# The second MLP product of a decoder layer as seven block products instead of eight

## What is computed

```
x = _layer_norm(ALPHA * x + mixed, ln1_g, ln1_b)
h = jnp.square(jax.nn.relu(jnp.einsum('bsd,df->bsf', x, w_up)))          # 512 x 4096
x = _layer_norm(ALPHA * x + jnp.einsum('bsf,fd->bsd', h, w_down), ln2_g, ln2_b)
```

## Time and profile before

| | |
|---|---|
| median of 3 runs | 865.61 us (865.6 to 865.99) |
| span of the profiled execution | 865.2 us |
| TensorE busy | 850.2 us (98%), 4185 matmuls |
| VectorE busy | 412.9 us (48%) |
| ScalarE busy | 295.9 us (34%) |
| GpSimd busy | 20.5 us (2%) |
| DMA | 87.42 MB, mean 101 GB/s |
| mean granted TensorE clock | 0.989 of full speed |

### The profile page before, as it was taken

How to read it: one execution, slowest core, us unless ns; L and a number is a source line. 1 busy time by engine, 2 the same in 40 slices (tenths; PEclk the granted TensorE clock), 3 DMA queues, 4 the chain that set the end, 5 groups by cost and what they waited for, 6 DMA issues and landing times.

```text
span 865.2 us, 10456 instructions
## 1 busy us (share of the span) xinstructions
PE 850.2 (98%) x4185; PEld 719.4 (83%) x4185; DVE 412.9 (48%) x481; ACT 295.9 (34%) x342; POOL 20.5 (2%) x30
## 2 busy tenths in 40 slices
PE   6999999999999999999999999999999999999996
PEld 6989888898888888888888899888888888888885
DVE  3737544566355514414427676513551355135554
ACT  3748323494036223222233134402440244024400
POOL 1200100000001000000000000000000000000000
PEclk9999989999799999999999999999999999999999
DMA  9631212312112322322724033403340334133211
GB/s 322 198 114 50 98 49 90 105 48 97 48 48 95 100 98 97 97 97 97 291 97 140 6 99 134 135 24 98 121 140 32 96 113 141 38 93 105 93 49 48
DMA packets 67088, 87.42 MB, mean 101 GB/s; under 512 B 1485, under 2 KB 50678, under 8 KB 67062
## 3 DMA queue, kind: packets, MB, share of 16 engines
q1 hardware_dynamic: 67062, 87.06, 30.3%
HBM read 84.96 MB, written 2.10 MB: 101 GB/s over the span
## 4 chain that ended last, share of the span: by engine, by line
PE 97%; DMA 1%; DVE 1%; ACT 0%; DVEq 0%; issue 0%
PE bank L1018 31%; PE bank L1019 30%; PE bank L1020 30%; PE bank L1161 2%; DMA raw<-in_w_mem_v_dram 1%; PE bank L1156 1%; DMA two<-in_mem_dram 1%; PE bank L1189 0%; PE bank L1124 0%; PE bank L1248 0%; PE bank L1039 0%; PE bank L1192 0%; PE bank L1179 0%; DVE w_lo L630 0%; DVE w_lo L625 0%; ACT w_hi L390 0%
## 5 line engine op out<-in xcount | busy, mean ns | idle before, releaser
L1018 PE MATMUL bank<-x_hi,w_hi 128*128 128x512 f32 (+1 forms) x704 | 269.9, 383 | 0.0
L1019 PE MATMUL bank<-x_lo,w_hi 128*128 128x512 f32 (+1 forms) x704 | 268.6, 382 | 0.0
L1020 PE MATMUL bank<-x_hi,w_lo 128*128 128x512 f32 (+1 forms) x704 | 268.5, 381 | 0.0
L625 DVE TENSOR_TENSOR w_lo<-raw,w_hi 128x2048 fp32r<-128x2048 f32 x73 | 166.5, 2291 | 150.5 <-ACT w_hi L390 150.2
L390 ACT ACTIVATE w_hi<-raw 128x2048 fp32r<-128x2048 f32 x73 | 138.5, 1911 | 171.1 <-PE bank L1020 142.1
L1020 PEld LDWEIGHTS bank<-x_hi,w_lo 128*128 128x128 f32 x704 | 133.3, 189 | 25.4
L1018 PEld LDWEIGHTS bank<-x_hi,w_hi 128*128 128x128 f32 x704 | 133.6, 190 | 24.9
L1019 PEld LDWEIGHTS bank<-x_lo,w_hi 128*128 128x128 f32 x704 | 133.5, 190 | 24.8
L1018 PE MATMUL bank<-w_hi,y_hi 128*128 128x512 f32 (+1 forms) x352 | 133.9, 380 | 0.4 <-DVE w_lo L625 0.4
L1020 PE MATMUL bank<-w_hi,y_lo 128*128 128x512 f32 (+1 forms) x352 | 133.6, 379 | 0.0
L1019 PE MATMUL bank<-w_lo,y_hi 128*128 128x512 f32 (+1 forms) x352 | 133.5, 379 | 0.0
(11 more groups left out here) (158 smaller groups left out, 648.7 us busy)
## 6 DMA issues: line engine op xcount, KB each, us to landing
raw<-in_w_in_dram SPq DMA_DIRECT2D x28, 1024.0 KB, 5.0
raw<-in_w_up_dram SPq DMA_DIRECT2D x16, 1024.0 KB, 6.2
raw<-in_w_down_dram SPq DMA_DIRECT2D x16, 1024.0 KB, 5.0
raw<-in_w_branch_dram SPq DMA_DIRECT2D x6, 1024.0 KB, 5.0
two<-in_x_dram SPq DMA_DIRECT2D x2, 2048.0 KB, 12.4
raw<-in_w_o_dram SPq DMA_DIRECT2D x4, 1024.0 KB, 5.0
raw<-in_w_mem_v_dram SPq DMA_DIRECT2D x2, 1024.0 KB, 8.2
out_dram<-two SPq DMA_DIRECT2D x8, 256.0 KB, 2.0
```

The source lines that it names most:

```text
L625: dve.tensor_tensor(w_lo[:, slot, :], raw[:, r, :], w_hi[:, slot, :].bitcast(F32), ALU.subtract)\
L1018: pe.matmul(dst, a[0], b[0], start=first, stop=False)
L1019: pe.matmul(dst, a[0], b[1], start=False, stop=False)
L1020: return pe.matmul(dst, a[1], b[0], start=False, stop=last)
```

## The change

The second product H·W of each group is done as a two-by-two block scheme with seven products (Strassen type). The blocks of H are (tokens 0 to 255, tokens 256 to 511) x (even, odd blocks of 128 features); the blocks of W are (even, odd feature blocks) x (columns 0 to 511, 512 to 1023). Each product is 256 tokens x 512 features x 512 columns: 2 tiles (r = 0, 1), each 4 k-steps x 3 = 12 matmuls of 512 columns. A group now has 7 x 2 x 12 = 168 matmuls for down instead of 192.

- Weights: of the seven weight operands three are plain blocks (m1, m3, m2), four are sums. SyncE loads the two starting blocks into `raw_a` and `raw_b` (parts of `small`); GpSimd adds further blocks of w_down on top of them by accumulating DMAs (`add_block`, two DMAs of 512 KB for 1 MB), each started when VectorE has split the previous content. `raw_a` serves m1, then (first add) m5, (second add) m6, (third add) m4; `raw_b` serves m3, then (add) m7. A group splits 11 slabs instead of 8.
- Activations: after each pair of up tiles ScalarE writes relu and square into `h_forms` and `h_kept`, VectorE makes four combinations of 128 x 256 (`forms`), ScalarE rounds six forms (one instruction of 128 x 1536, `forms_to_hi`) and VectorE writes the rest (`forms_lo`). There is one `h_forms` buffer: the next pair's even tile waits for `forms_ready`.
- Order on ScalarE per pair j: both tiles of pair j, then the split of product j's weights (`down_hi`, which waits for the landing of the add), then `forms_to_hi`. On VectorE: `forms`, `down_lo`, `forms_lo`.
- Results: products continue in the same bank where a running sum is wanted (banks 4 and 5 for m1, m6, m7, m4; 6 and 7 for m5, m3; 0 and 1 for m2), and VectorE adds or subtracts each of the 14 tiles of a group into the residual (`down_add`). A product may start in its bank only when VectorE has read the one before.
- The last group's LayerNorm: token blocks 2 and 3 are complete after m2 (their last product), blocks 0 and 1 only after m4, the last product. The stores follow in the order 2, 3, 0, 1.
- The loops over groups are unrolled.

The core of the diff:

```diff
-S_MLP, N_MLP = S_OUT + 4, 8
+S_MLP, N_MLP = S_OUT + 4, 11
+PRODUCTS = ("m1", "m5", "m6", "m3", "m2", "m7", "m4")
+DOWN_BANK = dict(m1=4, m6=4, m7=4, m4=4, m5=6, m3=6, m2=0)
+LAST_READ = dict(m6="m1", m7="m6", m4="m7", m3="m5")
...
@@ sync
+            for g in range(G_MLP):
+                up_load(g, 0)
+                up_load(g, 1)
...
+                    sp.wait_ge(slab_lo, down_slab(g - 1, "m4") + 1)
+                sp.dma_start(as_block(raw_a), down_block(g, 1, 1)).then_inc(a_landed, 16)
...
+                sp.dma_start(as_block(raw_b), down_block(g, 2, 2)).then_inc(b_landed, 16)
+                up_load(g, 2)
+                up_load(g, 3)
+                direct(g, 4, down_block(g, 2, 1), PAIRS)
@@ gpsimd
+            def add_block(buf, block, added):
+                for part in (slice(0, 2), slice(2, 4)):
+                    pool.dma_start(as_block(buf)[:, part], block[:, part], accum_op=ALU.add).then_inc(added, 16)
+            for g in range(G_MLP):
+                pool.wait_ge(slab_lo, down_slab(g, "m1") + 1)
+                add_block(raw_a, down_block(g, 1, 2), a_added)
+                pool.wait_ge(slab_lo, down_slab(g, "m5") + 1)
+                add_block(raw_a, down_block(g, 2, 2), a_added)
+                pool.wait_ge(slab_lo, down_slab(g, "m6") + 1)
+                add_block(raw_a, down_block(g, 2, 1), a_added)
+                pool.wait_ge(slab_lo, down_slab(g, "m3") + 1)
+                add_block(raw_b, down_block(g, 1, 2), b_added)
@@ scalar
+            def even_tile(g, j):
+                n = 8 * g + 2 * j
+                act.wait_ge(up_done, n + 1)
+                if n:
+                    act.wait_ge(forms_ready, n // 2)
...
+                for j in range(PAIRS):
+                    even_tile(g, j)
+                    odd_tile(g, j)
+                    if j < 3:
+                        down_hi(g, PRODUCTS[j])
+                    forms_to_hi(g, j)
+                down_hi(g, "m3")
+                down_hi(g, "m2")
...
+                down_hi(g, "m7")
+                down_hi(g, "m4")
@@ vector
+            def forms(g, j):
+                dve.wait_ge(h_squared, 8 * g + 2 * j + 2)
+                a21, a11, a12, m5, m7, m6, m3 = (h_forms[:, n, :] for n in range(7))
+                dve.tensor_tensor(m7, a11, a21, ALU.subtract)
+                step(dve.tensor_tensor(m5, a21, h_kept[:, j, :], ALU.subtract))
+                step(dve.tensor_tensor(m6, m5, a11, ALU.subtract))
+                dve.tensor_tensor(m3, m6, a12, ALU.add).then_inc(forms_made, 1)
...
+                for j in range(PAIRS):
+                    forms(g, j)
+                    if j < 3:
+                        down_lo(g, PRODUCTS[j])
+                    forms_lo(g, j)
+                down_lo(g, "m3")
+                for name in ("m1", "m5"):
+                    for r in range(2):
+                        down_add(g, name, r)
+                down_lo(g, "m2")
...
+                down_add(g, "m6", 0)
+                down_lo(g, "m7")
+                down_add(g, "m6", 1)
+                down_add(g, "m3", 0)
...
+                down_lo(g, "m4")
+                down_add(g, "m3", 1)
...
+                else:
+                    up_lo(g + 1, 0)
+                down_add(g, "m2", 0)
+                if last:
+                    half_stats(g, "m2", 0)
+                    norm_two(0, 2)
+                down_add(g, "m2", 1)
+                if last:
+                    half_stats(g, "m2", 1)
+                else:
+                    up_lo(g + 1, 1)
+                for r in range(2):
+                    down_add(g, "m7", r)
+                if last:
+                    norm_two(1, 3)
+                    half_stats(g, "m7", 0)
+                    half_stats(g, "m7", 1)
+                else:
+                    up_lo(g + 1, 2)
+                for r in range(2):
+                    down_add(g, "m4", r)
+                    if last:
+                        half_stats(g, "m4", r)
+                        norm_two(2 + r, r)
@@ tensor
+            def down(g):
+                for name in ("m1", "m5"):
+                    slab(down_slab(g, name))
+                    for r in range(2):
+                        down_ready(g, name, r)
+                        for j in range(PAIRS - 1):
+                            pe.wait_ge(forms_ready, PAIRS * g + j + 1)
+                            down_part(g, name, r, (j,))
+                pe.wait_ge(forms_ready, PAIRS * (g + 1))
+                for name in ("m1", "m5"):
+                    for r in range(2):
+                        down_part(g, name, r, (PAIRS - 1,)).then_inc(down_done, 1)
+                for name in PRODUCTS[2:]:
+                    slab(down_slab(g, name))
+                    for r in range(2):
+                        down_ready(g, name, r)
+                        down_part(g, name, r, range(PAIRS)).then_inc(down_done, 1)
```

More of the change, by code:

```diff
@@ new lines, in down_hi @@
+            def down_hi(g, name):
+                p = PRODUCTS.index(name)
+                if p < UP_SLABS:
+                    act.wait_ge(up_done, 8 * g + 2 * p + 2)
+                else:
+                    act.wait_ge(down_done, made(g, PRODUCTS[p - 4], 1))
+                if name == "m2":
+                    direct_hi(g, 4)
+                    return
+                if name == "m1":
+                    act.wait_ge(a_landed, 16 * (g + 1))
+                elif name == "m3":
+                    act.wait_ge(b_landed, 16 * (g + 1))
+                elif name == "m7":
+                    act.wait_ge(b_added, 32 * (g + 1))
+                else:
+                    act.wait_ge(a_added, 32 * (3 * g + ("m5", "m6", "m4").index(name) + 1))
+                split(down_slab(g, name), raw_b if name in ("m3", "m7") else raw_a)
@@ L617, in _ @@
+            for g in range(G_MLP):
+                mlp(g)
         @block.vector
@@ L998, in _ @@
+            for g in range(G_MLP):
+                mlp(g, g == G_MLP - 1)
         @block.tensor
@@ L1308, in _, with up_tile @@
-            mlp(0, 2)
-            with pe.Fori(1, G_MLP) as g:
-                mlp(g)
+                feature_part(bank[u], slice(T // 2, T), u // 2, u % 2).then_inc(up_done, 1)
+            def up_tile(g, u):
+                n = 8 * g + u
+                pe.wait_ge(up_read, n - MAIN + 1)
+                if g and u < 2:
+                    pe.wait_ge(down_read, made(g - 1, "m2", u))
+                s = S_MLP + g * N_MLP + u // 2
+                if u % 2 == 0:
+                    slab(s)
+                feature_part(bank[u % MAIN], slice(0, T), (s - S_MLP) % 4, u % 2).then_inc(up_done, 1)
@@ new lines, in down_part @@
+            def down_part(g, name, r, pairs):
+                dst = bank[DOWN_BANK[name] + r]
+                slot = (down_slab(g, name) - S_MLP) % 4
+                for j in pairs:
+                    mm = three(dst, both(form_hi, form_lo, ALL, FORM_OF[name],
+                                         slice(j * 256 + r * P, j * 256 + (r + 1) * P)),
+                               w_part(slot, j * WID, WID), name in DOWN_OPENS and j == 0, j == PAIRS - 1, name not in DOWN_OPENS)
+                return mm
@@ L1314 @@
+            for g in range(G_MLP):
+                for u in range(MAIN if g == 0 else 0, 8):
+                    up_tile(g, u)
+                down(g)
 _INS = ["x", "mem", "lower_bounds", "w_in", "conv_w", "hg_norm_w", "w_mem_k", "w_mem_v", "w_branch", "b_gate",
```

255 lines of the change are left out of this document (163 added, 92 removed).

## The result

The changed kernel takes 917.23 us (915.45 to 919.23, 4 runs) against 865.61 (864.38 to 865.99, 4 runs): ratio 1.0613, 95% interval 1.0574 to 1.0651. Slower by 6%, where 852.5 was forecast with a range up to 872. The profiled execution has a span of 915.3 us.

What follows compares the result with a forecast made beforehand. TensorE's matmuls were taken to bound the MLP: span 865.2 - 21.8 (matmuls) + 4.4 (end) + 3.4 + 0.4 + 0.5 (waits) = 852.1, plus 0.4 from span to median, 852.5 us. The range was 847 to 872.

Steps and rivals of the forecast that it cites:

- L: Time from the start of a 1 MB weight add (two DMAs of 512 KB) to its landing, taken as 8.0 us.
- The bounds (5.1 and 12.9): Ends for L: a plain 1 MB load, 5.1 us, and the slowest load in the middle of the trace, 12.9 us.
- the prediction's sum: Whole span: 865.2 less 21.8 for matmuls, plus 4.4 at the end, plus waits growing with L; 852.1 at L = 8.
- Removed matmuls: Four MLP groups: 24 of 384 matmuls fewer in each, at 0.2267 us, 21.8 us gained.
- pace: MLP matmuls keep their shape and should stay 0.2267 us apart.
- the hidden work of VectorE and ScalarE: Added work per group beside TensorE: VectorE 50 us of 81.6, ScalarE 38 us, neither a bound by its sum.
- unrolled loops: Edges between groups: straight code costs nothing, since TensorE shows no idle time there.
- The end: After the last matmul: two LayerNorms left, VectorE ending 9.0 us after the last tile is readable, 4.4 us more than before.
- The chain arithmetic: Up stage, wait for the last pair's forms: 2L - 12.6 in the first group (3.4 us), 2L - 17.6 in others.
- the rule L - 7.5: Ahead of m4, TensorE waits for m7's first tile to be read: 0.5 us at L = 8.
- The rival with a long L: Adds in the up stage take 9.4 us or more, say 10, giving 871.9, slower than before; chance 0.24.
- Held-up descriptors: Rival at the adds GpSimd issues: descriptors are held up and the kernel becomes slower; chance 0.05.

Runs made afterwards that it cites:

- short loads: Changed kernel with the adds replaced by plain 1 MB loads issued by SyncE at the same points, weight sums left out: 848.63 us, span 846.8.

## Why the prediction was wrong

The step that failed is the size of L. The prediction took 2.5 us fixed, 2 x 2.6 us of bytes and 0.3 to 0.4 us for the second issue. The first two were nearly right: with both halves in flight, or as one DMA, an add mostly lands after 8.1 to 8.6 us, up to 0.6 more than taken. The third was not 0.4 but 6.2 us (528.84 to 535.04): the second half was issued only when the first had landed (534.78). With `dynamic_dma_scratch_size` at 2048 instead of 1024, and nothing else changed but the place of two masks, both halves of the first add were issued within 2.62 us, and the time fell by 41 us. Why the size does this, no run shows. I had priced the issue by SyncE's 0.37 us, the issue of another engine (GpSimd's take 1.20 to 1.37 us for 512 KB), and treated two DMAs as one with a small addition. The bounds (5.1 and 12.9) did hold 11.9, though not the fourth add's 14.8; the value between them, and with it the range up to L = 10, did not. The change had left a hint that I did not weigh: it cuts a 1 MB transfer in two for no reason that the code shows, beside a parameter of 1024 bytes in the launch code.

L is not all of it. With L at 8.5 (the change's own order, each add one DMA) the prediction's sum gives a span of 853.6; measured were 863.8, no faster than the kernel before. TensorE waits 12.5 us there, where the sum has 5.8, and 27 slow matmuls cost 5.6 us, where it has nothing. So two terms more were wrong: the clock was priced at nothing, and the wait ahead of m4 was taken as none in the groups where the forms are in time up to L = 8.8, and as none at all in the last group. It was 2.2, 1.1 and 2.9 us in the three later groups of that run, and about 5 in the last group of the change.

Step by step:

- Removed matmuls, pace, the hidden work of VectorE and ScalarE, unrolled loops: right. With short loads the span was 846.8 against 847.8.
- The end: 4.4 us more forecast, 4.2 more with short loads. In the changed kernel it is 2.3, since VectorE had time during m4's wait; with that wait filled it was 3.9.
- The chain arithmetic: right in size with the measured L. First group 549.0 + 23.2 - 561.6 = 10.6 us of wait at m1, measured 10.7; second group 11.6 + 11.2 - 17.6 = 5.2, measured 5.3. The place was off by one pair: the wait is for the third pair's forms. Counted there the formula is 541.5 + 23.2 - 554.8 = 9.9, the last 0.7 us having stood at the fourth pair; the slow matmuls behind the wait covered that. Ahead of m4 the rule L - 7.5 gives 7.3 with the fourth add's 14.8 us, measured 5.9 to 6.0 in each of the first three groups (0.9 to 1.0 at the slab, 5.0 at m4).
- The rival with a long L had the right mechanism and side, at L = 10 and 871.9. At L = 12 its sum gives a span of 893.5. In TensorE's time the 22 us from there to 915.3 are 20.4 of slow clock and 5.4 of waits beyond the sum's 45.7 (nearly all of it the wait ahead of m4 in the last group), less 2.1 at the end and 2.8 because the MLP began earlier; 1.0 is left over. What set them is known in part: the filled pauses put 2.2 to 2.7 us of slow clock a group on the path, and the fourth add took 14.8 us instead of 12 in three groups. How the rest divides isn't settled.
- Held-up descriptors (the chance of 0.05), read as issues by GpSimd that last longer beside VectorE's work: not seen. In the changed kernel the first issue takes 1.37 us and all others 1.20 to 1.24, those beside `forms_lo` (545.39) like those beside an idle VectorE (551.14). No run isolates it.

One link of the loop, in the changed kernel's chain that ended last (start, length, what):

```profile
526.22 2.30 DVE w_lo L757
528.53 0.31 issue
528.84 1.37 POOL small L451
530.21 4.83 issue
535.04 5.65 DMA small<-in_w_down_dram
540.78 1.93 ACT w_hi L660
542.73 2.30 DVE w_lo L757
```

Of a link of 16.5 us, 4.83 is the pause in the issue and 5.65 the second half. TensorE isn't in this link at all.

## What to carry to other kernels

A DMA of a kind that the trace doesn't hold has a price of its own, and several of them in a row have one more, since they may not overlap (here the second half came 6.2 us behind the first, and a size of 2048 instead of 1024 in the launch code put both within 2.6 us); look for a split or a size in the code that such a limit would explain. When an added transfer sits in a chain behind one buffer, work out up to what length the slack covers it, and put nothing that the bounding engine needs behind it in an in-order queue; but follow what the new order delays, since one order tried here only moved the wait to m7. When the price of one step has been put right, redo the whole sum: here the right L alone would have left the forecast 10 us too low. A pause of the bounding engine can cost more than its length (here 2.4 us of slow matmuls behind a pause of 5.0 to 10.7 us), but only where that engine is on the loop: filling the pause tells where.

## What the hardware showed that was not expected

- GpSimd's second accumulating DMA of 512 KB waited 4.4 to 5.8 us in its issue with 1024 as `dynamic_dma_scratch_size`. With 2048 or 1536 most pairs were both issued within 2.4 to 2.6 us and an add mostly took 8.1 to 8.6 us; which ones still wait follows a pattern that repeats in each group and was not explained (2048: the second add's half; 1536: the third's; one DMA of 1 MB with 2048: none, unless an add is already in flight).
- With 2048 bytes an add of 1 MB that came while another was in flight was held in its issue until that one had landed: GpSimd stood idle for that long (6.1 to 6.3 us behind two halves, 7.4 behind one DMA).
- Adding while landing cost 2.7 us for 1 MB over a plain copy from the same queue (8.4 against 5.7 us, medians of twelve; 2.2 in the first add).
- After the changed kernel's eight pauses of 5.0 to 10.7 us TensorE's granted clock was 0.50 for some 12 matmuls (0.427 us apart, 2.4 us lost); with matmuls filling all but the last 2 us of the first group's pause it stayed at 1.00.
